# First layer's values projected token-major, with the activations as the stationary operand, in groups of four banks

## The reference

```
def attention_mixer(hn, w_in, ...):            # hn: 512 tokens x 1024
    z = hn @ w_in                               # w_in: 1024 x 3080
    dq, dk, dv, fq, fk, fv, fz = jnp.split(z, idx, axis=-1)   # six of 512 columns, fz of 8
    d_out = differential_attention(dq, dk, dv, lam)   # 4 heads, values of 128 columns
    f_out = forgetting_attention(fq, fk, fv, cumsum(log_sigmoid(fz + b)))   # 8 heads of 64
    return concat(d_out, f_out) @ w_out
```

## Time and profile before

| | |
|---|---|
| median of 3 runs | 3394.43 us |
| lowest, highest | 3387.39, 3395.04 us |
| the profiled execution: time, and span from first to last instruction | 3385.32, 3383.6 us |
| mean granted TensorE clock of the profiled execution | 0.902 of full |
| PE busy | 2872.8 us (85%) |
| DVE busy | 1017.4 us (30%) |
| ACT busy | 375.9 us (11%) |
| POOL busy | 254.3 us (8%) |

### The profile page before, as it was taken

How to read it: one execution, slowest core, us unless ns; L and a number is a source line. 1 busy time by engine, 2 the same in 40 slices (tenths; PEclk the granted TensorE clock), 3 DMA queues, 4 the chain that set the end, 5 groups by cost and what they waited for, 6 DMA issues and landing times.

```text
span 3383.6 us, 22234 instructions
## 1 busy us (share of the span) xinstructions
PE 2872.8 (85%) x8331; PEld 1348.9 (40%) x8331; DVE 1017.4 (30%) x1999; ACT 375.9 (11%) x855; POOL 254.3 (8%) x299
## 2 busy tenths in 40 slices
PE   7988889999899887999998997747779996767765
PEld 3444334444354333444443383324444444323222
DVE  4135244300324143123003218765550014000002
ACT  1014100000110311000001000002550001000001
POOL 1000000000000000000000303330000000111211
PEclk9989999999989978999999969877999996877877
DMA  3310146522212112222213321001002233566452
GB/s 103 80 45 19 50 140 190 158 76 65 65 50 75 47 38 75 75 75 75 81 37 93 84 74 27 19 13 38 1 1 66 74 124 132 230 244 240 181 226 108
DMA packets 345318, 303.80 MB, mean 90 GB/s; under 512 B 32284, under 2 KB 323025, under 8 KB 332511
## 3 DMA queue, kind: packets, MB, share of 16 engines
q1 hardware_dynamic: 325116, 260.18, 24.3%
q0 software_dynamic: 19584, 40.32, 3.8%
q10 hardware_dynamic: 528, 2.10, 0.2%
HBM read 346.13 MB, written 16.78 MB: 107 GB/s over the span
## 4 chain that ended last, share of the span: by engine, by line
PE 73%; DVE 11%; ACT 5%; DMA 5%; issue 3%; POOL 1%; SPq 0%; POOLq 0%; DVEq 0%; ACTq 0%
PE bank L1346 54%; ACT work L1570 4%; DMA work<-expert_in_scratch,small 4%; PE bank L655 4%; PE bank L1357 3%; PE bank L1438 2%; PE bank L527 1%; PE bank L622 1%; PE bank L1390 1%; PE bank L489 1%; PE bank L517 1%; DVE rinv L1745 1%; PE bank L1364 1%; PE bank L635 1%; PE bank L1420 1%
## 5 line engine op out<-in xcount | busy, mean ns | idle before, releaser
L1346 PE MATMUL bank<-xnT,ring 128*128 128x512 f32 (+2 forms) x2400 | 1048.7, 599 | 36.8 <-DVE xnT L1752 30.2
L1346 PE MATMUL bank<-big,ring 128*128 128x512 f32 x1728 | 760.3, 601 | 49.0 <-DVE big L2032 28.9
L1346 PEld LDWEIGHTS bank<-xnT,ring 128*128 128x128 f32 (+2 forms) x2400 | 457.2, 191 | 625.6 <-issue 620.5
L1346 PEld LDWEIGHTS bank<-big,ring 128*128 128x128 f32 x1728 | 330.9, 192 | 475.0 <-issue 455.7
L1570 ACT ACTIVATE work<-bank 128x512 f32<-128x512 f32 (+2 forms) x221 | 111.3, 544 | 763.8 <-PE bank L635 295.9
L655 PE MATMUL bank<-big,work 128*64 128x512 f32 x384 | 133.3, 858 | 26.6 <-ACT work L1570 25.6
L1570 ACT ACTIVATE work<-work,nmax 128x512 f32<-128x512 f32 (+1 forms) x192 | 105.4, 552 | 317.8 <-DVE nmax L1818 317.4
L2011 DVE TENSOR_SCALAR work<-bank 128x512 f32<-128x512 f32 x64 | 44.3, 692 | 300.6 <-PE bank L1346 300.6
L622 PE MATMUL bank<-ident,work 128*128 128x128 f32 x192 | 42.9, 395 | 107.2 <-DMA work<-expert_in_scratch,small 107.2
L2023 DVE COPY big<-bank 128x512 f32 x16 | 11.1, 692 | 399.4 <-ACT xnT L1570 399.3
L1420 PE MATMUL bank<-ident,work 128*128 128x128 f32 x440 | 71.1, 303 | 58.2 <-ACT work L1570 49.1
(11 more groups left out here) (325 smaller groups left out, 2370.5 us busy)
## 6 DMA issues: line engine op xcount, KB each, us to landing
ring<-in_mlp_w_up_dram SPq DMA_DIRECT2D x64, 512.0 KB, 4.0
ring<-in_mlp_w_down_dram SPq DMA_DIRECT2D x64, 512.0 KB, 4.1
big<-in_moe_w_down_dram SPq DMA_DIRECT2D x32, 1024.0 KB, 7.0
work<-in_ada_w_dram POOLq DMA_DIRECT2D x32, 768.0 KB, 4.6
ring<-in_w_in_dram SPq DMA_DIRECT2D x40, 512.0 KB, 3.8
big<-in_moe_w_gate_dram SPq DMA_DIRECT2D x16, 1024.0 KB, 8.6
big<-in_moe_w_up_dram SPq DMA_DIRECT2D x16, 1024.0 KB, 10.6
ring<-in_moe_w_gate_dram SPq DMA_DIRECT2D x16, 1024.0 KB, 11.2
```

The source lines that it names most:

```text
L1346: ins = pe.matmul(bank[0:m, 0:n], w[:, q, :], rhs(k), start=(k == 0), stop=(k == total - 1))
```

## The change

The 8 value tiles leave `QKV0`. For each of the two value groups (`A_DV`, `A_FV`), PE opens all four banks, one for each 128 tokens; a chunk now holds 2 k-tiles of all 512 value columns (rows of 512 floats, 2 KB, still 512 KB per chunk), and for each k-tile PE runs four matmuls, with a 128x128 piece of `xnT` stationary and the 128x512 weights moving, one into each bank. The result is token-major. The 8 `turn4` and their copies go, `mT` is no longer written here, and DVE copies the four banks of a group straight to `V0` once the group's last chunk is used. The rest of the diff keeps the counts of tiles and turns of the other engines in step.

```
-                + [A_FK + P * j for j in range(4)] + [A_DV + P * j for j in range(4)] + [A_FV + P * j for j in range(4)])
-        NQK = 17
+                + [A_FK + P * j for j in range(4)])
+        V_FROM = [A_DV, A_FV]
...
# SP
             for n0 in QKV0:
                 chunk(w_chunk(W["attn_w_in"], 0, KD, n0, width0(n0)), KD, width0(n0))
+            for n0 in V_FROM:
+                for j in range(4):
+                    chunk(w_chunk(W["attn_w_in"], 2 * j * P, 2, n0, T), 2, T)
...
# PE
-            for j in range(8):
-                evacuated(pe, tile0 + NQK + j)
-                turn4(lambda a: mT[:, j, a * P:(a + 1) * P])
+            for n0 in V_FROM:
+                to = [open_tile() for a in range(TT)]
+                for j in range(4):
+                    w = slot_view(take_chunk(), 2, T)
+                    for q in range(2):
+                        k = 2 * j + q
+                        for a in range(TT):
+                            ins = pe.matmul(to[a][:, :], xnT[:, k, a * P:(a + 1) * P], w[:, q, :], start=(k == 0), stop=(k == KD - 1))
+                    ins.then_inc(chunk_used, 1)
...
# DVE
-                elif j < NQK:
+                else:
                     free_bank(V.tensor_copy(big[:, j - 1, :], bank[:, :]), n)
-                else:
-                    free_bank(V.tensor_copy(mT[:, j - NQK, :], bank[:, :]), n)
...
-            for j in range(8):
-                n = take_turned()
-                free_bank(V.tensor_copy(V0[:, :, j // 4, (j % 4) * P:(j % 4 + 1) * P], bank_of(n)[:, :].rearrange("p (a n) -> p a n", a=TT)), n)
+            for g in range(2):
+                ct.chunk += 4
+                dve.wait_ge(chunk_used, ct.chunk)
+                for a in range(TT):
+                    free_bank(V.tensor_copy(V0[:, a, g, :], bank_of(ct.tile)[:, :]), ct.tile)
+                    ct.tile += 1
```

More of the change, by code:

```diff
@@ L286, in model_kernel @@
         N_WIN2 = len(WIN2)
-        WIN1_TILE = [1 + KD + len(QKV0) + 16 + N_DIFF + KD + (32 + 8 + 2 + 2 * KD) * 2 + 2 * KR + 2 * KR + KD + 1]
+        WIN1_TILE = [1 + KD + len(QKV0) + 8 + 8 + N_DIFF + KD + (32 + 8 + 2 + 2 * KD) * 2 + 2 * KR + 2 * KR + KD + 1]
         def kv_slot(branch, h):
@@ L1473, in _ @@
             before = new_xn()
-            tile0 = ct.tile
             for j, n0 in enumerate(QKV0):
                 dense_tile([KD], lambda k: xnT[:, k, :], m=width0(n0), before=before if j == 0 else None)
-            for j in range(8):
-                evacuated(pe, tile0 + NQK + j)
-                turn4(lambda a: mT[:, j, a * P:(a + 1) * P])
+            for n0 in V_FROM:
[7 more added lines that the diff above has]
+                    ins.then_inc(chunk_used, 1)
             pe.wait_ge(sem("log_forget"), 1)
@@ L1645, in _ @@
             act_(FZ[2], FZ[1], ACT.Exp, scale=-1.0).then_inc(sem("forget_exp"), 1)
-            ct.chunk, ct.tile = len(QKV0), ct.tile + len(QKV0) + 16
+            ct.chunk, ct.tile = len(QKV0) + 8, ct.tile + len(QKV0) + 8 + 8
             attention(0, N_FIRST)
@@ L1666, in _ @@
                     act.wait_ge(sem("c4_ready"), 1)
-                    base_turned = 1 + KD + 8 + 8 + N_DIFF + 2
+                    base_turned = 1 + KD + 8 + N_DIFF + 2
                     for i in range(KR):
```

## The result

Over 12 runs each, the changed kernel takes 3393.11 us (3388.87 to 3396.92) and the kernel before 3386.24 us (3378.93 to 3395.04). The ratio is 1.0018, 95% interval 1.0010 to 1.0026: slower by some 6 us, under the 0.3% that the prediction set as the bound of "same", but beyond the interval. The three runs of before shown ahead of the prediction (median 3394.43) were high ones of their kind. So the forecast level of 3395.8 came close partly by luck: it stood on a level 8.2 us too high. What it said of the difference was +1.4 us, and +6 to +7 was measured.

The account below looks back on a forecast made before the run. The prediction took PE, busy 2872.8 of 3383.6 us, as the bound. Its terms, +0.90 + 2.73 + 0.9 - 3.13 = +1.4 us, on the median of the runs before (3394.43) gave 3395.8 us, range 3383 to 3404.

Parts of the forecast that it names:

- The dense part stays; no cost for banks taking turns: Value matmuls on PE: 64 per group, 54.9 us before and after; bank turns 0, upper bound 3.4 us.
- The weights' DMAs are worth nothing: Weight loads: still 8 issues of 512 KB, with 2 KB rows; faster rows only lengthen SP's wait for PE.
- (a): In front of the first value group PE waits for four banks, three long empty: +0.90 us.
- (b): Between the value groups PE waits until DVE has emptied all four banks: +2.73 us.
- (c): After the second value group the first gate matmul waits for a bank, one copy after the group's end: +0.90 us.
- The clock after wait (b): Second value group: half clock behind PE's idle time costs 0, 1.72 or at most 3.1 us; +0.9 us taken.
- The gate matmuls: Last value matmul to attention: clock falls 4.0 us after the first gate; end takes 11.84 us, -3.13 us.
- three readings: Clock's fall under the gates: 4.0 us after the first gate, or 8.0 or 2.9 after dense work; gains 3.13, 6.1, 1.2.
- Theory A: Made after the measurement: token-major form is free; bank waits, half clock behind the long one and 8-row gates without transposes cost.
- the clock falls at both waits: Rival, ahead of and between the value groups: half clock behind each wait, +3.9 us in sum, 3398.3 us; chance 0.18.
- price of 1.72 us: Loss to half clock behind an idle time, read from two such places in the third layer: 2.77 + 2.81 against 1.98 + 1.88.
- loads in the open: Rival, value matmuls: stationary loads not hidden, up to 0.19 us on each of 128 instructions, 24.3 us, 3419 us; chance 0.05.

Follow-up runs that it names:

- gates_among_keys: Changed kernel with one gate matmul behind each of the eight key tiles, waits for four banks kept; 3390.59 us, ratio to before 1.0011.
- experiment 5: Also bank_by_bank: changed kernel in which DVE empties each bank of a value group once that bank's last matmul is done; 3385.47 us, ratio to before 0.9994.
- two_bank_sets: Also experiment 1: changed kernel with the first value group in banks 4 to 7, the second in banks 0 to 3; 3384.56 us, ratio to before 0.9993.
- experiment 3: Changed kernel whose gate matmuls use all 128 rows, zeros below the 8 that count; 3384.79 us, ratio to before 0.9998.
- experiment 2: Same run as gates_among_keys: changed kernel with the eight gate matmuls moved among the key tiles, waits kept; 3390.59 us, ratio to before 1.0011.

## Why the prediction was right or wrong

The verdict "same" and the range held, but both were wide (0.3% is 10.2 us, the range 21 us). The size of the difference did not hold: +1.4 us was forecast, +6.1 (ratio) to +6.9 (medians) measured. By the prediction's own steps, from the trace of the changed kernel:

- *The dense part stays; no cost for banks taking turns.* Right. 64 instructions take 27.70 us at full clock. Only 0.24 us come in at the end of each group, where the last matmul runs out before DVE can begin; I had not counted these.
- *The weights' DMAs are worth nothing.* Right; SP waits for PE as before. The effect of the rows alone was not tried on the chip.
- *Waits (a) and (b) of 0.90 and 2.73 us, (c) of 0.90.* Right: 0.99, 2.78, 0.88.
- *The clock after wait (b), +0.9 us.* About half of what was paid. I had taken half of a choice between 0 and 1.72 us; 1.70 were paid in two of the three traces that have this wait and 3.05 in the third (gates_among_keys). A wait of 0.98 us in the same place cost nothing (experiment 5).
- *The gate matmuls, -3.13 us.* This is the step that failed. The end went from 14.97 to 0.88 + 12.66 + 0.90 = 14.44 us, a gain of 0.53. My premise was that the clock would fall 4.0 us after the first gate as before; it fell 1.4 us after it. Even the worst of my three readings (a gain of 1.2) was too good. In four traces with 8-row gates at the end it fell 4.0 (before), 1.4 (changed), 3.6 (two_bank_sets) and 5.5 us (bank_by_bank) after the first, so one trace could not have given a figure for it. How much the term is worth turns on this: with the fall after 3.6 us, in two_bank_sets, the same end takes 0.88 + 10.40 + 1.01 = 12.29 us, a gain of 2.68, near the forecast. Whether the transposes had held the clock up stays open, since without them it fell both sooner and later than with them; so does why it fell after 1.4 us in the changed kernel. What the runs do show is that the 8 rows are the condition: with 128 rows it did not fall in three traces.

With the measured terms: 0.99 + 2.78 + 1.70 - 0.53 = +4.9 us, and the two ends of groups make it 5.4, of 5.57 in the stretch. Theory A therefore holds in its parts, the word on the transposes excepted: taking the waits away (experiment 1, with a later fall under the gates beside it) or the clock's fall under the gates alone (experiment 3) each brings the kernel back to before. Of the rivals, "the clock falls at both waits" did not happen in the changed kernel but did in experiment 2, behind the same 0.99 us. The section "A second HAM failure mode: psum-queue depth-cycling" of the Trainium skill's page "TensorE: Matmul & The Clock Gate", named in the prediction, tells of a kernel that cycled through PSUM banks and whose clock went down and up between groups. The traces agree for the wait of 2.78 us (27.70 us became 29.40 and 30.75); behind 0.98 and 0.99 us between full-height matmuls, four times in three traces, the clock stayed up.

Two sums of the prediction are off, without weight. The price of 1.72 us adds two groups of instructions that overlap in the trace; from the first start to the last end it is 5.37 - 3.70 = 1.67 us. And the 3419 us of the loads in the open leave out the forecast's own +1.4.

## What to carry to other kernels

An operand swap that yields the wanted layout directly is free on the matmuls but not on the banks: a group that finishes several banks at once needs either a second set of banks or a reader that is told of each bank as it ends, or the next group waits for the whole burst of copies and may run at half clock behind it, as it did in all three traces with such a wait between the groups. Where small matmuls end a stretch of dense work, look at the granted clock under them: here the ones over 8 rows fell to half clock, and the same ones padded to full height with zeros did not. And three runs of the kernel before can mislead: here their median was 8.2 us above that of twelve, more than the effect.

## What the runs showed of the hardware

- Eight matmuls of 8 rows took 8.66 to 12.66 us at the end of the projection, with the granted clock falling to 0.50 under them in four traces out of four; the same eight with 128 rows, mostly zeros, took 7.03 to 7.11 us in three traces out of three, with the granted clock at 1.00 throughout.
- Behind a wait of 2.78 us between dense groups the granted clock went to 0.50 in three traces out of three, which cost 1.70, 1.70 and 3.05 us. Ahead of the scores of attention it went down behind 2.62 us in one trace and stayed at 1.00 behind 2.73 us in another. Behind 0.98 or 0.99 us between full-height matmuls it stayed at 1.00, four times in three traces; behind 0.99 us after an 8-row matmul it went down once, for 1.70 us.
- A float32 matmul of 8 rows and 512 columns between tiles of 128 rows lengthens the period by 1.25 us, one of 128 rows by 0.86, at full clock both.
